# First projection of each later stage queued chunk by chunk with the making of its input

## What is computed

```python
x = x + gate1 * y                                   # y: attention of this layer, projected
h = rmsnorm(x, norm2_g[i]) * (1.0 + scale2) + shift2
x = x + gate2 * swiglu(h, f_w_in[i], f_w_out[i])
...
h = rmsnorm(x, norm1_g[i]) * (1.0 + scale1) + shift1
y = diff_attention(h, ...)                          # i = 0: h @ w_qkv first
y = axial_gqa(h, ...)                               # i = 1: h @ w_qkv first
```

## Time and profile before

| | us |
|---|---|
| median of 3 runs | 1385.19 (1384.85 to 1385.59) |
| profiled execution, its own time | 1380.57 |
| profiled execution, span of the instructions | 1378.8 |
| TensorE matmul busy (share of the span) | 1148.3 (83%) |
| VectorE busy | 611.7 (44%) |
| ScalarE busy | 540.8 (39%) |
| mean granted TensorE clock | 0.942 of 2.4 GHz |

### The profile page before, as it was taken

The page is one execution under the profiler, slowest core; times in us unless marked ns, Lnnn a source line. Parts: engine busy times, 40 slices in busy tenths (PEclk is TensorE's granted clock), DMA queues, the critical chain, the costliest instruction groups (busy, mean ns, idle before and its releaser), DMA issues.

```text
span 1378.8 us, 22374 instructions
## 1 busy us (share of the span) xinstructions
PE 1148.3 (83%) x9627; PEld 916.8 (66%) x9627; DVE 611.7 (44%) x1363; ACT 540.8 (39%) x1203; POOL 0.2 (0%) x4
## 2 busy tenths in 40 slices
PE   6989998866656666555689989999999979999997
PEld 4867668543333444333357758899998758899997
DVE  4564664210100111110065756665555865655554
ACT  4554553211100110110154655555554754555553
POOL 0000000000000000000000000000000000000000
PEclk9999998998887898987899999999999999999999
DMA  9895846899999999999978646645545664655520
GB/s 392 340 357 222 350 190 244 332 427 428 428 424 428 424 427 427 427 426 427 428 311 323 217 182 224 247 182 184 184 145 210 235 236 183 245 184 184 184 92 31
DMA packets 29569, 397.53 MB, mean 288 GB/s; under 512 B 3480, under 2 KB 4888, under 8 KB 5400
## 3 DMA queue, kind: packets, MB, share of 16 engines
q1 hardware_dynamic: 29032, 395.72, 71.8%
q10 hardware_dynamic: 432, 0.30, 0.1%
HBM read 394.97 MB, written 1.05 MB: 287 GB/s over the span
## 4 chain that ended last, share of the span: by engine, by line
PE 58%; DMA 24%; DVE 9%; ACT 7%; issue 2%; ACTq 0%; DVEq 0%
PE ps L141 58%; DMA ring<-in_w 12%; DMA mem<-in_w 11%; DVE mem L141 4%; DVE memr L141 3%; ACT mem L141 3%; ACT memr L141 3%; DMA ring<-in_wpk 1%; DVE small L141 1%; DMA posi<-in_pos 1%; ACT L141 0%; ACT rowb L141 0%; DVE x L141 0%; DVE mcol L141 0%; ACTq L141 0%
## 5 line engine op out<-in xcount | busy, mean ns | idle before, releaser
L141 PE MATMUL ps<-memr 128*128 128x256 f32 (+1 forms) x4680 | 668.6, 302 | 17.9 <-DVE memr L141 17.9
L141 PEld LDWEIGHTS ps<-memr 128*128 128x128 f32 x4680 | 610.7, 192 | 62.4 <-DVE memr L141 27.7
L141 DVE TENSOR_TENSOR memr<-ring,memr 128x512 fp32r<-128x512 f32 x440 | 297.8, 691 | 245.3 <-ACT memr L141 242.0
L141 ACT ACTIVATE memr<-ring 128x512 fp32r<-128x512 f32 x440 | 268.3, 627 | 220.0 <-PE ps L141 212.3
L141 PE MATMUL ps<-mem 128*32 128x256 f32 (+4 forms) x2232 | 266.8, 407 | 59.9 <-DMA mem<-in_w 35.2
L141 ACT ACTIVATE mem<-ps 128x256 f32<-128x256 f32 (+5 forms) x307 | 121.3, 407 | 421.4 <-PE ps L141 419.4
L141 PEld LDWEIGHTS ps<-mem 128*32 128x32 f32 (+2 forms) x2232 | 172.8, 147 | 117.8 <-issue 59.5
L141 PE MATMUL ps<-ring,mem 128*32 128x256 f32 x1536 | 140.6, 432 | 75.6 <-DMA mem<-in_w 39.0
L141 PEld LDWEIGHTS ps<-ring,mem 128*32 128x32 f32 x1536 | 72.2, 124 | 122.4 <-issue 99.3
L141 DVE TENSOR_TENSOR mem<-mem,ps 128x256 f32<-128x256 f32 (+1 forms) x76 | 31.8, 418 | 270.7 <-ACT mem L141 270.6
L141 DVE COPY mem<-ps 32x256 f32<-32x256 f32 (+2 forms) x81 | 38.2, 471 | 114.9 <-PE ps L141 113.9
(11 more groups left out here) (91 smaller groups left out, 380.4 us busy)
## 6 DMA issues: line engine op xcount, KB each, us to landing
ring<-in_wpk SPq DMA_DIRECT2D x89, 2048.0 KB, 8.1
mem<-in_w SPq DMA_DIRECT2D x48, 2048.0 KB, 32.0
ring<-in_w SPq DMA_DIRECT2D x48, 2048.0 KB, 30.4
mem<-in_wpk SPq DMA_DIRECT2D x1, 2048.0 KB, 10.5
ring<-in_wpk SPq DMA_DIRECT2D x2, 1024.0 KB, 5.1
x<-in_x SPq DMA_DIRECT2D x2, 512.0 KB, 5.6
out_dram<-mem SPq DMA_DIRECT2D x4, 256.0 KB, 2.2
cst<-in_cst SPq DMA_DIRECT2D x1, 944.0 KB
```

The lines of the kernel that those rows point to most:

```text
L141: ins = o[1](*o[2], **o[3])
```

## The change

It makes the generator `project_steps` out of `project`, and lets `modulate_x` take a `first` function. After each `low`, one step of the first product is queued at once: its matmuls, `slab_done` with at most one slab staged, and after chunk 2 `ada_close(True)`. `project` and `project_T` take a product that is begun from the list `begun` and only finish it. `use_tables(SILU)` before the feed-forward loop goes, so that the table is loaded by the first `silu`. In the expert stage `hold` is dropped early, and at a chunk where no slab is ahead one is staged.

```diff
--- before.py
+++ after.py
@@ -322,6 +322,7 @@
         sp_free = [[] for _ in range(NSP)]
         sp_rec = [None] * NSP
         side = []
+        begun = []
 
         def stage(most=NSP):
 
@@ -339,7 +340,8 @@
                     load_unit(state["slot"][n], [sp_rec[z]])
 
         def slab():
-            stage()
+            if st["made"] == st["used"]:
+                stage(1 if begun else NSP)
             assert st["made"] > st["used"]
             z = st["used"] % NSP
             return (sp[:, z, 0, :], sp[:, z, 1, :]), sp_rec[z], z
@@ -460,10 +462,10 @@
             mm(out, a[0], b[1], False, False)
             return mm(out, a[1], b[0], False, stop)
 
-        def project(x2, x_r, evac, order=tuple(range(8))):
+        def project_steps(x2, x_r, out):
 
             bk = [PB.take(), PB.take()]
-            for kk, k in enumerate(order):
+            for kk, k in enumerate(range(8)):
                 w, ld, z = slab()
                 for tt in range(2):
                     s = slice(128 * tt, 128 * tt + 128)
@@ -472,6 +474,15 @@
                 slab_done(z, r)
                 if kk == 2:
                     ada_close(True)
+                yield
+            out.extend([bk, r])
+
+        def project(x2, x_r, evac):
+
+            g, out = begun.pop(0) if begun else (None, [])
+            for _ in g or project_steps(x2, x_r, out):
+                pass
+            bk, r = out
             outs = []
             for tt in range(2):
                 v = evac(tt, bk[tt][1], [r])
@@ -497,8 +508,9 @@
             out.extend([bk, r])
 
         def project_T(x2, x_r, c1, c2):
-            out = []
-            for _ in project_T_steps(x2, x_r, c1, c2, out):
+
+            g, out = begun.pop(0) if begun else (None, [])
+            for _ in g or project_T_steps(x2, x_r, c1, c2, out):
                 pass
             return out
 
@@ -576,7 +588,7 @@
         def gcol_of(i, half):
             return ([C_N1, C_N1B, C_N1B + 8] if half == 0 else [C_N2, C_N2B, C_N2B + 8])[i]
 
-        def modulate_x(i, half, rB_r, x_r, hooks={}, scale=None, plain=False, recs=None):
+        def modulate_x(i, half, rB_r, x_r, hooks={}, scale=None, plain=False, recs=None, first=None):
             held, frees = None, list(h2_free)
             recs = {} if recs is None else recs
             rB_free.clear()
@@ -587,6 +599,11 @@
                 recs[c] = V(vt.scalar_tensor_tensor, out=h2[1][:, c, :], in0=uu[:, z, :], scalar=sh,
                             in1=h2[0][:, c, :], op0=ALU.add, op1=ALU.subtract, after=[ra])
                 uu_free[z] = [recs[c]]
+                if first:
+                    if c == 0:
+                        out = []
+                        begun.append((first(h2, recs, out), out))
+                    next(begun[0][0])
 
             for c in range(8):
                 z = c % 3
@@ -604,6 +621,7 @@
                       in1=rB, op0=ALU.mult, op1=ALU.mult, after=[rB_r, a_r, x_r[c]] + uu_free[z])
                 rB_free[:] = [r]
                 if plain:
+                    st["hold"] = False
                     recs[c] = A(sc.activation, hT[:, c, :], uu[:, z, :], ACT.Identity, bias=sh, after=[r] + frees)
                     uu_free[z] = [recs[c]]
                     continue
@@ -611,11 +629,11 @@
                 if held:
                     low(*held)
                 held = (c, z, sh, ra)
-                if split and 0 < c < 4:
-                    stage(1)
-                if c == 1 and not split:
+                if c == 1 and st["hold"]:
                     st["hold"] = False
                     stage()
+                elif st["used"] == st["made"] or (split and 0 < c < 4):
+                    stage(1)
             if held:
                 low(*held)
             return recs
@@ -1565,7 +1583,7 @@
         r = A(sc.activation, rB, ps[:, 0:256], ACT.Ln, bias=EPS * EPS, scale=1.0 / D, after=[r])
         PB.give(b, [r])
         rB_r = A(sc.activation, rB, rB, ACT.Exp, scale=-0.5, after=[r])
-        h2_r = modulate_x(1, 0, rB_r, x1_r, {3: ada_copy}, scale=am1_r)
+        h2_r = modulate_x(1, 0, rB_r, x1_r, {3: ada_copy}, scale=am1_r, first=project_steps)
         r = A(sc.activation, lam[:, 0:2], lam[:, 0:2], ACT.Exp, after=[lam_in])
         lam_r = V(vt.scalar_tensor_tensor, out=lam[:, 2:3], in0=lam[:, 1:2], scalar=-LAM_INIT, in1=lam[:, 0:1],
                   op0=ALU.add, op1=ALU.subtract, after=[r])
@@ -1873,8 +1891,8 @@
             ada_mm(*extra_u[0])
             rB_r = nm.close()
             ada_mm(*extra_u[1])
-            h2_r = modulate_x(i, 1, rB_r, x_r, {3: ada_copy})
-            use_tables(SILU)
+            h2_r = modulate_x(i, 1, rB_r, x_r, {3: ada_copy},
+                              first=lambda x2, recs, out: project_T_steps(x2, recs, 128, 256, out))
             f_r = []
             g_fr = [[c_last] for _ in range(4)]
             for n in range(11):
@@ -1914,7 +1932,7 @@
             rB_r = nm.close()
             if i == 1:
                 ada_mm(2, 5)
-                h2_r = modulate_x(2, 0, rB_r, x_r, {3: ada_copy})
+                h2_r = modulate_x(2, 0, rB_r, x_r, {3: ada_copy}, first=project_steps)
 
         ov = t["out"]
         fo = []
```

## The result

The changed kernel takes 1453.2 us (median of 5 runs, 1448.7 to 1456.2) against 1385.19: a ratio of 1.0483 with the 95% interval 1.0465 to 1.0500, so 68.0 us longer. The profiled execution took 1453.2, its span is 1451.4 us.

A forecast was written before the change was run, and what follows sets the result against it. TensorE was taken to set the pace, with VectorE having little room at stage starts. Queueing of 51.5 us plus 26.4 us for the clock made 77.9, added to 1385.2 for 1463 us, range 1435 to 1475.

The forecast's parts named there:

- The turn: Feed-forward starts: chunk matmuls, slab copy, slab rest and next chunk's operations follow each other, 3.99 us per chunk instead of 1.39.
- After the experts: Stage start after the experts: no copy waits for the last chunk, but VectorE and ScalarE alternate, 2.18 us per chunk.
- The table load: Behind the last copy, its 1.28 us lie beside a chunk of the next product, so it costs nothing.
- the second norm costs nothing: Its VectorE work moves one product later, beside TensorE-bound chunks with 0.7 us to spare each, so no cost.
- The 51.5 us of queueing: Loss without the clock: 29.8 for two feed-forward starts, 16.0 before the second attention, 5.7 after the experts and at program start.
- losses of 14.9 and 16.0: Later start of chunk 7: 14.9 us in each feed-forward part, 16.0 us before the second attention.
- 5.7: Loss in us after the experts, given as 4.2 plus 0.7 for the next product, with 0.4 at the program's beginning.
- The clock's term: TensorE's clock falls to 1.2 GHz in the three long stages, costing 26.4 us, with bounds 0 and 38.5.
- stays down until the stage ends: In each of three long stages the clock falls early and does not recover before the end, 8.8 us a stage.
- no return with pauses: Earlier trace row, 2.11 us busy in 323 to 327 at clock 0.50, taken as showing pauses prevent the clock's return.
- the copies do not bite (1397): Rival: turns only alternate ScalarE and VectorE, 2.18 us each, because the slab is a chunk older; 12 us loss, chance 0.06.
- the clock stays up (1437): Rival: clock stays at 2.4 GHz in the long stages, loss 51.5 us; chance 0.17, including a fall in only some stages.

## Why the prediction was right

**The direction and the mechanism** hold step by step. The turn was forecast as 3.99 and is 3.90 to 3.94 at full clock (the copy starts 1.70 after a chunk that stands alone, not 1.79). The kernel with a buffer kept free shows that this wait is the cause, and the extra matmuls show its size without the clock: 27.5 to 27.75 us from chunk 0 to chunk 7. **After the experts** the forecast was 3.1 to chunk 0, 2.18 a turn, 3.3 for the long turn and 16.0 in all; measured 3.21, 2.18, 3.41 and 16.1. The whole stage lost 3.4 against 4.9: at the end of its attention the clock had fallen for 3.4 us before and did not after. **The table load** costs nothing in its new place, as forecast: it stands at 908.81, inside an unbroken run of TensorE from 906.42 over 19.3 us. That the second norm costs nothing was not looked at by any run. The load alone is a gain, which the forecast could not see within this change, because the wait it filled is gone with the old order.

**The 51.5 us of queueing** seem to be met by 1436.4 - 1385.7 = 50.7 with the clock held up, but that is luck in part. 2.9 of the 50.7 are the extra matmuls' own time, so queueing cost 47.8. The traces agree: 14.3 in each feed-forward start, 15.6 before the second attention and 4.4 after the experts make 48.6. The forecast was 3 to 4 us too high. Its losses of 14.9 and 16.0 are 0.6 and 0.4 too large: a chunk was taken as 1.39 us, where the starts of chunks 5, 6 and 7 in the trace before are 1.44 apart, so that chunk 7 came 13.45 us after chunk 0 and not 13.2, and the new turns are 3.90 to 3.94. Its 5.7 is also added up wrongly, for 4.2 + 0.7 + 0.4 are 5.3, and of the 0.7 the trace shows 0.1 (3.41 us from chunk 7 to the next product's first chunk, 3.30 before).

**The clock's term was mis-sized.** The step "stays down until the stage ends", 8.8 us a stage and 26.4 in all, measured about 20: 68.0 less the 47.8 of queueing. In the traces, the starts with the change are 4.7, 6.6 and 5.1 us longer from chunk 0 to chunk 7 than those with the extra matmuls. Before the second attention the low clock lasted 4 us beyond chunk 7's start, some 2 us more, and the fall at 1157.8 may add up to 1.7. The 10 us by which 1463 is too high are these 6 us and the 4 of queueing. A turn at the low clock was forecast as 5.2, and the first such turn took 5.13. The fall came in all three stages, at the first turn. What failed is the staying down: the clock was at half for 17.1, 30.7 and 20.5 us of the three starts, with returns between.

The row that was to show "no return with pauses" (323 to 327) was misread. The same trace has no pauses there, but one long wait and then work without a break, in which the clock came back (at 330.8). One row of the timeline and three windows of TensorE in the kernel before:

```profile
324.89 0.64 PE L141 MATMUL ps<-ring,mem 128*32 128x256 f32 x2 [7.16 <-DMA mem<-in_w]
327.00:331.00 4.00, 4.00 (x44) 0.53 1.00 426
371.10:375.10 4.00, 2.20 (x32) 1.00 1.01 426
375.10:379.10 4.00, 3.53 (x32) 0.57 1.01 430
```

The last two windows weaken the other reading of the earlier trace rows as well. A stretch with 2.20 us busy in 4 was followed by a fall, although the one with 2.13 (1102) was not. So those rows gave less ground for the fall than the prediction says, and that it was right there owes something to luck.

**The rule on idle gaps.** The Trainium skill (TensorE: Matmul & The Clock Gate, Why this matters for your kernels) warns there only of long gaps. Here the clock fell with pauses of 2.24 us (the rows above). The measurement decides against reading that rule as a licence for shorter pauses.

**The rivals.** That the copies do not bite (1397) is what the kernel with the free buffer became, 1396.2, with the turns of 2.18 us that this rival names; in the change itself they bit. The closeness of the number is luck, for the rival's terms 2 x 2.3 + 3.7 + 5.7 make 14.0 us and not 12, so 1399. That the clock stays up (1437) needed the extra matmuls (1436.4).

## What to carry to other kernels

In a queue that is worked off in order, ask of each waiting instruction what stands behind it, not only what it waits for: a prefetch into a ring that is full waits for the work just queued, and whatever is queued behind the prefetch joins that wait. If consumers are queued early, keep the prefetches in the producers' lists at least one buffer away from the newest consumer: here that took the turn from 3.90 to 2.18 us. With the copy also ahead of the operations that need another engine's answer it was 1.40. And a chain that let TensorE rest for 2.24 us of each 3.90 cost twice: 48 us by the rest, then 20 by the clock.

## What was not expected of the hardware

The granted clock went up again inside a stage with a pause of more than 2 us in each turn. In the first feed-forward part with the change it was at 0.50 from 877.9 to 881.3, from 888.2 to 895.0 and from 898.4 to 905.2, and at 1.00 between, although every chunk in the first of these stretches (one of 2.89 us) and in the second (the end of one and one of 2.93) stood alone. In the second feed-forward part with the late reduces it stayed at 0.50 for 34 us with the same chunks of 2.93 us and the same pauses. With the change it lay at 0.50 over 1233 to 1246, where a chunk and the transposes make 4.6 us in one piece, and was back at 1.00 over 1247 to 1253. So a longer piece of work is not needed for the return, and whether it helps is not shown. The fall varied too: with the late reduces it came at the first turn in one stage and only at chunk 3 in the two others. These traces show that the same code can meet either, and not what decides it. An estimate of such a cost needs a wide range.
